# Gate products of the even layer as three fp32r products, their operands split on ScalarE, GpSimd and VectorE; ring loads and two copies moved ahead

## The reference, cut to what matters

```python
uh = uf.reshape(bsz, seq, RG_HEADS, RG_HEAD_DIM)          # 8 heads of 128 channels
gates = jax.nn.sigmoid(jnp.einsum('bshi,ghij->gbshj', uh, gate_w) + gate_b)
r, i = gates[0], gates[1]                                  # for each of two directions
log_a = -RG_C * r * jax.nn.softplus(-lam)
a = jnp.exp(log_a)
b = jnp.sqrt(-jnp.expm1(2.0 * log_a)) * (i * uf)
h = scan(a, b)                                             # forward, and in reverse
ya = (h_forward + h_reverse) * silu(za)
yb = gb * centred_dwconv(gc * xb, sc_w) * silu(zb)
y = concatenate([ya, yb]) @ w_out
```

## Time and profile before

| | us |
|---|---|
| median of 3 runs | 2738.15 |
| lowest and highest run | 2737.18, 2739.89 |
| the profiled execution's own time | 2736.76 |
| its span, first to last instruction | 2734.9 |
| PE busy in the span | 2696.8 (99%) |
| POOL, DVE, ACT busy | 1624.7, 1356.1, 708.7 |

### The profile page before, as it was taken

One profiled execution on the slowest core, in us unless ns is written; L12 is line 12 of the kernel. 1 busy time (PEld: TensorE's weight loads), 2 busy tenths in 40 slices (PEclk: granted clock), 3 DMA queues, 4 the chain that ended last, 5 costly groups with the idle time before them and its releaser, 6 DMA issues.

```text
span 2734.9 us, 36055 instructions
## 1 busy us (share of the span) xinstructions
PE 2696.8 (99%) x13190; PEld 2166.0 (79%) x13190; DVE 1356.1 (50%) x1605; ACT 708.7 (26%) x1235; POOL 1624.7 (59%) x949
## 2 busy tenths in 40 slices
PE   9999999999999999999999999999999999999999
PEld 6777777877888888867888888788888766888887
DVE  7878824574432461176440454642246777543242
ACT  4443423343200110284210113310012476211010
POOL 5666755524665666603665665566666799566565
PEclk9999999999999999999999999999999999999999
DMA  4222222202332322301332332333232100233232
GB/s 180 101 97 91 89 93 86 84 24 75 94 115 77 98 95 93 93 8 47 93 110 83 100 100 92 124 100 113 80 100 92 55 1 2 85 100 115 77 98 87
DMA packets 62028, 235.58 MB, mean 86 GB/s; under 512 B 6880, under 2 KB 7008, under 8 KB 61792
## 3 DMA queue, kind: packets, MB, share of 16 engines
q1 hardware_dynamic: 61920, 234.14, 26.9%
HBM read 232.02 MB, written 2.10 MB: 86 GB/s over the span
## 4 chain that ended last, share of the span: by engine, by line
PE 80%; DVE 6%; POOL 4%; PEld 3%; ACT 2%; issue 2%; DVEq 1%; DMA 1%; PEldq 0%; POOLq 0%; ACTq 0%; SPq 0%
PE ps L364 23%; PE ps L366 23%; PE ps L365 23%; POOL arena L2458 4%; PE ps L388 1%; PE ps L382 1%; PE ps L383 1%; PE ps L1045 1%; PEld ps L712 1%; PEld ps L713 1%; PEld ps L714 1%; PE ps L1029 1%; POOL w_lo L334 0%; DVE w_tails L1828 0%; DMA ring<-in_even_in 0%
## 5 line engine op out<-in xcount | busy, mean ns | idle before, releaser
L334 POOL TENSOR_TENSOR w_lo<-ring,w_hi 128x1024 fp32r<-128x1024 f32 (+2 forms) x382 | 985.9, 2581 | 56.5 <-issue 3.1
L332 POOL CAST w_hi<-ring 128x1024 fp32r<-128x1024 f32 (+2 forms) x382 | 435.1, 1139 | 910.7 <-PE ps L366 724.8
L364 PE MATMUL ps<-hi,w_hi 128*128 128x512 f32 x2064 | 809.0, 392 | 5.3 <-POOL w_lo L334 2.4
L365 PE MATMUL ps<-lo,w_hi 128*128 128x512 f32 x2064 | 803.2, 389 | 0.0
L366 PE MATMUL ps<-hi,w_lo 128*128 128x512 f32 x2064 | 803.2, 389 | 0.0
L364 PEld LDWEIGHTS ps<-hi,w_hi 128*128 128x128 f32 x2064 | 387.4, 188 | 93.1 <-POOL w_lo L334 6.0
L365 PEld LDWEIGHTS ps<-lo,w_hi 128*128 128x128 f32 x2064 | 387.5, 188 | 81.9 <-issue 2.1
L366 PEld LDWEIGHTS ps<-hi,w_lo 128*128 128x128 f32 x2064 | 387.4, 188 | 80.8
L364 PE MATMUL ps<-hid_hi,w_hi 128*128 128x512 f32 x704 | 274.4, 390 | 0.0
L365 PE MATMUL ps<-hid_lo,w_hi 128*128 128x512 f32 x704 | 274.0, 389 | 0.0
L366 PE MATMUL ps<-hid_hi,w_lo 128*128 128x512 f32 x704 | 273.9, 389 | 0.0
(11 more groups left out here) (367 smaller groups left out, 3318.8 us busy)
## 6 DMA issues: line engine op xcount, KB each, us to landing
ring<-in_ffn_in SPq DMA_DIRECT2D x176, 512.0 KB, 3.6
ring<-in_even_in SPq DMA_DIRECT2D x48, 512.0 KB, 4.9
ring<-in_ffn_out SPq DMA_DIRECT2D x32, 768.0 KB, 4.3
ring<-in_ffn_out SPq DMA_DIRECT2D x32, 640.0 KB, 3.9
ring<-in_even_out SPq DMA_DIRECT2D x16, 512.0 KB, 3.6
ring<-in_sb_qk SPq DMA_DIRECT2D x12, 512.0 KB, 3.6
ring<-in_odd_v SPq DMA_DIRECT2D x8, 512.0 KB, 3.6
ring<-in_odd_r SPq DMA_DIRECT2D x8, 512.0 KB, 3.7
```

The lines of the kernel that those rows point to most:

```text
L332: nc.gpsimd.tensor_copy(high[:, j % 2, 0:cols], ring[:, j, 0:cols])
L334: nc.gpsimd.tensor_tensor(low[:, j % 2, 0:cols], ring[:, j, 0:cols], high[:, j % 2, 0:cols].bitcast(F32), ALU.subtract).then_inc(sem["w_re ...
L364: nc.tensor.matmul(bank, w_hi[:, j % 2, w], x_hi[:, k, :], start=(k == 0), stop=False)
L365: nc.tensor.matmul(bank, w_hi[:, j % 2, w], x_lo[:, k, :], start=False, stop=False)
```

## The change

Three things are done, all in the even layer.

1. **Weights ahead of gate tiles.** In SP's loop the wait for `even_channel_done` and the load of the gate tile move from ahead of a channel's six slots to behind the fourth (`n == RING`).
2. **Two copies ahead of the roots.** In the first channel ACT moves banks 2 and 3 for the second channel (its `xa` and `xb`) ahead of the first channel's two square roots instead of behind them.
3. **Gates as three fp32r products.** ACT rounds the gate tile (`gw_hi`, 128x512) one channel ahead, and rounds `ua` (`ua_hi`, 128x512) behind its move of the fifth bank. POOL subtracts to get `gw_lo`, in two halves of 128x256, each behind a split of a slot. DVE subtracts to get `ua_lo` (128x512), behind the first instruction of the other branch (in the last channel directly behind `ua`, in the first behind its extra work). PE then has 12 fp32r matmuls per channel instead of 4 with unrounded operands, and waits for `ua_low` and for both halves (`gates_split`).

The core of the diff:

```diff
@@ -425,6 +425,12 @@
         nsp = r.take(16)
         nsp_c = r.tiles(2, 2)
         lt = r.tiles(6, 16)
+        r.at = (r.at + P - 1) // P * P
+        gw_hi = [at(f"gw_hi_{jj}", 4 * P, start, F32R) for jj, start in enumerate((ARENA_AT + r.at, place["root"]))]
+        r.take(4 * P)
+        gw_lo = tiled("gw_lo", 2, GATE_COLS, ARENA_AT + 16 * T, F32R)
+        ua_hi = at("ua_hi", T, place["acc"], F32R)
+        ua_lo = at("ua_lo", T, place["ring"] + 3 * SLOT + 8 * P, F32R)
         even_tmp = [ps[:, 4 + d, :] for d in range(2)]
         rinv_even = ps[:, 6, :]
 
@@ -612,10 +618,11 @@
                     with sp.Fori(0, RG_HEADS // 2 - 1) as i:
                         for jj in range(2):
 
-                            sp.wait_ge(sem["even_channel_done"], 2 * i + (jj + 3))
-                            gate_weight(i + 1, jj)
                             for n in range(6):
                                 s = 6 * jj + n
+                                if n == RING:
+                                    sp.wait_ge(sem["even_channel_done"], 2 * i + (jj + 3))
+                                    gate_weight(i + 1, jj)
                                 sp.wait_ge(sem["w_ready"], 12 * i + (s + 13))
                                 even_weight(i + 1, s)
                     continue
@@ -657,12 +664,14 @@
 
             def even_gates(i, jj):
 
-                pe.wait_ge(sem["ua_ready"], 2 * i + (jj + 1))
+                pe.wait_ge(sem["gates_split"], 4 * i + (2 * jj + 2))
                 pe.wait_ge(sem["gates_read"], 2 * i + (jj + 1))
-                pe.wait_ge(gate_landed[jj], 16 * i + 16)
+                pe.wait_ge(sem["ua_low"], 2 * i + (jj + 1))
                 for g in range(4):
-                    mm = nc.tensor.matmul(ps[:, 4 + g, :], gw[:, jj, g * P:(g + 1) * P], ua[:, jj, :],
-                                          start=True, stop=True)
+                    w = slice(g * P, (g + 1) * P)
+                    nc.tensor.matmul(ps[:, 4 + g, :], gw_hi[jj][:, w], ua_hi[:, :], start=True, stop=False)
+                    nc.tensor.matmul(ps[:, 4 + g, :], gw_lo[:, jj, w], ua_hi[:, :], start=False, stop=False)
+                    mm = nc.tensor.matmul(ps[:, 4 + g, :], gw_hi[jj][:, w], ua_lo[:, :], start=False, stop=True)
                 mm.then_inc(sem["gates_done"], 1)
 
             def even_channel(i, jj, c=None):
@@ -1311,18 +1320,28 @@
             rinv_act(act, "even_pre")
             nc.scalar.activation(rinv_even, root[:, :], ACT.Exp, scale=-0.5).then_inc(sem["rinv_copied"], 1)
 
+            def even_move(i, jj, n, c=None):
+                dst, func = [(xa_pad[:, jj, 2:2 + T], ACT.Copy), (xb_s[:, jj, :], ACT.Copy), (gc_s[:, jj, :], ACT.Copy),
+                             (gb_s[:, jj, :], ACT.Copy), (szb[:, jj, :], ACT.Silu), (sza[:, jj, :], ACT.Silu)][n]
+                s = 6 * jj + n
+                if c == 0:
+                    act.wait_ge(sem["plain_scaled"], n + 1)
+                else:
+                    act.wait_ge(sem["slots_used"], 12 * i + used("even_in", s + 1))
+                nc.scalar.activation(dst, ps[:, s % RING, :], func).then_inc(sem["even_moved"], 1)
+
+            def gates_high_act(i, jj):
+                act.wait_ge(gate_landed[jj], 16 * i + 16)
+                nc.scalar.activation(gw_hi[jj][:, :], gw[:, jj, 0:4 * P], ACT.Copy).then_inc(sem["gates_high"], 1)
+
             def even_act(i, jj, c=None):
                 act.wait_ge(sem["even_channel_done"], 2 * i + (jj + 1))
 
-                dsts = [(xa_pad[:, jj, 2:2 + T], ACT.Copy), (xb_s[:, jj, :], ACT.Copy), (gc_s[:, jj, :], ACT.Copy),
-                        (gb_s[:, jj, :], ACT.Copy), (szb[:, jj, :], ACT.Silu), (sza[:, jj, :], ACT.Silu)]
-                for n, (dst, func) in enumerate(dsts):
-                    s = 6 * jj + n
-                    if c == 0:
-                        act.wait_ge(sem["plain_scaled"], n + 1)
-                    else:
-                        act.wait_ge(sem["slots_used"], 12 * i + used("even_in", s + 1))
-                    nc.scalar.activation(dst, ps[:, s % RING, :], func).then_inc(sem["even_moved"], 1)
+                for n in range(2 if c == 1 else 0, 6):
+                    even_move(i, jj, n, c)
+                    if n == (1 if c == 0 else 4):
+                        act.wait_ge(sem["ua_ready"], 2 * i + (jj + 1))
+                        nc.scalar.activation(ua_hi[:, :], ua[:, jj, :], ACT.Copy).then_inc(sem["ua_high"], 1)
                     if c == 0 and n == 3:
                         for k in range(DT):
                             act.wait_ge(sem["even_scaled"], k + 1)
@@ -1331,6 +1350,8 @@
                     y_highs(DT, 2 * DT - 1)
                     act.wait_ge(sem["even_channel_done"], 1 + RG_HEADS)
                     y_highs(0, DT - 1)
+                else:
+                    gates_high_act(i + jj, 1 - jj)
                 par = gw[:, jj, 4 * P:4 * P + 16]
                 act.wait_ge(sem["gates_done"], 2 * i + (jj + 1))
                 for d in range(2):
@@ -1347,6 +1368,9 @@
                 for d in range(2):
                     a = nc.scalar.activation(hg[d], rg[d], ACT.Tanh, scale=nsp_c[:, jj, d:d + 1])
                 a.then_inc(sem["decay_ready"], 1)
+                if c == 0:
+                    even_move(0, 1, 0)
+                    even_move(0, 1, 1)
                 if c == RG_HEADS - 1:
                     act.wait_ge(sem["yb_done"], 1)
                     y_highs(2 * DT - 1, 2 * DT)
@@ -1359,6 +1383,7 @@
                     x_hi = hi[:, k, :] if k < DT else lo[:, k - DT, :]
                     nc.scalar.activation(x_hi, y_even[:, k, :], ACT.Copy).then_inc(sem["y_high"], 1)
 
+            gates_high_act(0, 0)
             for jj in range(2):
                 even_act(0, jj, jj)
             with act.Fori(0, RG_HEADS // 2 - 2) as i:
@@ -1768,6 +1793,10 @@
                 if c != 0:
                     V.tensor_copy(nsp_c[:, jj, :], nsp2[:, 2 * i + jj, :])
 
+                def ua_lower():
+                    dve.wait_ge(sem["ua_high"], 2 * i + (jj + 1))
+                    V.tensor_tensor(ua_lo[:, :], ua[:, jj, :], ua_hi[:, :].bitcast(F32), ALU.subtract).then_inc(sem["ua_low"], 1)
+
                 scale_plain(0)
                 scale_plain(1)
                 moved(1)
@@ -1777,11 +1806,14 @@
                     op = V.scalar_tensor_tensor(ua[:, jj, :], xa_pad[:, jj, k:k + T], par[:, 4 + k:5 + k],
                                                 ua[:, jj, :], ALU.mult, ALU.add)
                 op.then_inc(sem["ua_ready"], 1)
+                if c == RG_HEADS - 1:
+                    ua_lower()
 
                 if c == 0:
                     scale_plain(2)
                     scale_plain(3)
                     normed(0, DT)
+                    ua_lower()
                     scale_plain(4)
                     scale_plain(5)
                     decay_terms((11, 9, 7, 5, 3, 1))
@@ -1800,6 +1832,8 @@
                 moved(3)
                 V.tensor_tensor(u_pad[:, 1:1 + T], gc_s[:, jj, :], xb_s[:, jj, :], ALU.mult)
                 dve.drain()
+                if c not in (0, RG_HEADS - 1):
+                    ua_lower()
                 V.tensor_scalar(cv, u_pad[:, 0:T], par[:, 9:10], None, ALU.mult)
                 for k in range(1, 3):
                     dve.drain()
@@ -2388,9 +2422,22 @@
             pool.wait_ge(sem["w_ready"], ready("even_in", 1))
             for j in range(1, RING):
                 split_slot(pool, "even_in", 0, j)
-            with pool.Fori(0, slots_of["even_in"] // RING - 1) as i:
-                for j in range(RING):
-                    split_slot(pool, "even_in", i + 1, j)
+            def split_gates(i, jj, half):
+                w = slice(2 * P * half, 2 * P * half + 2 * P)
+                pool.wait_ge(sem["gates_high"], 2 * i + (jj + 1))
+                pool.sem_inc(sem["split_begun"], 1)
+                nc.gpsimd.tensor_tensor(gw_lo[:, jj, w], gw[:, jj, w], gw_hi[jj][:, w].bitcast(F32), ALU.subtract)\
+                    .then_inc(sem["gates_split"], 1)
+
+            for s in range(RING, 12):
+                split_slot(pool, "even_in", s // RING, s % RING)
+                if s in (5, 6, 10, 11):
+                    split_gates(0, s // 8, s % 5 % 2)
+            with pool.Fori(0, RG_HEADS // 2 - 1) as i:
+                for s in range(12):
+                    split_slot(pool, "even_in", 3 * i + (3 + s // RING), s % RING)
+                    if s % 6 in (2, 3):
+                        split_gates(i + 1, s // 6, s % 6 - 2)
             pool.wait_ge(sem["consts_landed"], 16)
             for dst, name in ((ident_1, "ident"), (causal_1, "causal_neg"), (sb_neg_1, "sb_neg"), (neg_c_1, "neg_c")):
                 G.tensor_copy(dst, con(name))
```

(2 more changed lines are left out.)

## The result

The changed kernel takes 2783.82 us (median of 5 runs, 2783.44 to 2784.86), against 2738.22 for the kernel before, timed beside it: a ratio of 1.0167, 95% interval 1.0156 to 1.0178. It is 45.6 us slower. The forecast said slower by 17; its range ended at 2771.

The account below looks back on a forecast made before the run. PE bounds the kernel, with DVE, alternating with POOL, a second clock. Stretches +9.2, -0.2, +6.5, +2.0 and last gates -0.4 gave +17.1 on 2736.76, 2753.9; with 1.4 for the median, 2755 us, slower by 0.6%; range 2739 to 2771.

Parts of the forecast that it names:

- PE, 2.72 us for the gates: Gate products on PE: 12 matmuls take 2.72 us against 3.44, 0.72 less per channel, 5.8 in all.
- SP: Wait moved behind the fourth slot: ring stays full, removing PE's waits for `w_lo` (2.2 and three of 0.5).
- The two copies count nothing: First stretch: copies remove its 1.6 us stall, but DVE holds the second gate start; counted nothing, bound 0 to 1.6.
- ACT's copy of the gate tile is free: ACT's gate-tile copy falls into its wait for the gates, free; if ACT were full, 0.60 us a channel.
- The halves, 0.7: POOL's two halves per channel delay DVE by 0 to 1.2 us; 0.7 taken.
- the 35.8 of the forecast: Steady period: `ua` ready 35.8 us behind the gate start, from 33.64, gates -0.72, a fifth slot subtraction 2.2, halves 0.7.
- First stretch 41.5: First to second gate start: 41.5 us through added DVE and POOL work, against 32.3, so +9.2.
- Steady period 38.1: Later gate starts 38.1 us apart by DVE's path; PE, ready at 35.4, waits 2.7 in every channel.
- rival D: One collision more: POOL's next-slot subtraction also precedes `ua_lo`, 2.3 us more in six periods, 13.8: 2769; chance 0.17.
- No term for the clock: Ahead of each gate call: PE waits 2.7 us, counted with no charge for the clock.
- The estimate made from it: Gates on PE: four passes at this pace give 3.63 us, gain 0.91 a channel, 7.3 in all; sum used the row's 3.44.

Follow-up runs that it names:

- e6: Changed kernel with 20 spare matmuls ahead of PE's wait for `ua_lo` in channels 1 to 6: 2771.65 us against 2737.47, ratio 1.0117.
- e1: Kernel before with only SP's wait and gate-tile load moved behind the fourth slot: 2741.87 us against 2737.47, ratio 1.0016.
- e2: Kernel before with only ACT's two copies of channel 1 moved behind the decay of channel 0: 2737.96 us against 2737.47, ratio 1.0000.
- e11: Changed kernel without the move of ACT's two copies, both other parts kept: 2781.37 us (2 runs), ratio 1.0158.
- e4: Changed kernel without POOL's two gate halves from channel 2 on, PE multiplying by `gw_hi` instead: 2752.11 us (2 runs), ratio 1.0050.
- e5: Changed kernel without DVE's subtraction that makes `ua_lo` in channels 2 to 5, semaphore raised in its place: 2767.75 us (2 runs), ratio 1.0107.
- e7: Changed kernel with `ua_lo` directly behind `ua` in every channel but the first: 2768.23 us (2 runs), ratio 1.0109.
- e8: e7 with POOL starting the first slot of a channel only behind `ua_ready`: 2741.20 us against 2738.32 (11 runs), ratio 1.0009.
- e10: e8 with the cast of a channel's first slot on ACT and POOL's subtraction behind `ua_lo`, replacing the `ua_ready` waits: 2739.37 us against 2737.43, ratio 1.0006.
- e9: Kernel before, unrounded gates, with weights ahead, copies ahead and POOL's two waits for `ua_ready`: 2735.59 us against 2737.43 (11 runs), ratio 0.9991.
- e12: e10 with ACT's cast also for the output projection's first slot, and 20 spare matmuls ahead of the second gate start: 2735.66 us against 2737.91, ratio 0.9991.
- e3: Changed kernel with SP's wait and the copies put back, so only the three-product gates are new: 2741.16 us against 2737.47, ratio 1.0012.

## Why the prediction was wrong in size

The direction was right, and so was the place. The sum was short by 29.9 us (2783.82 against 2753.9 for the profiled execution). By its own steps:

- *PE, 2.72 us for the gates*: near right wherever the clock was up (2.72 in the first channel, 2.88 from 177.61 to 180.49 in e6), but 4.2 to 5.3 in the changed kernel's other channels.
- *SP*: right. The ring is full and the waits for `w_lo` are gone (e1).
- *The two copies count nothing*: right as far as e2 and e11 can tell.
- *ACT's copy of the gate tile is free*: no run speaks against it; the copy of `ua` took 0.63 us.
- *The halves, 0.7*: mis-sized. Their own length in alternation is 1.19 each (rows of after above), and they push `ua` back. `ua` came 36.55 us behind the gate start in e6 (173.31 less 136.76) and 35.09 without the halves in e4: they cost 1.46, over the upper bound of 1.2. Without them the forecast's sum is 35.1, and e4 meets it. The 0.7 us that the term was short decide more than their size, since they decide on which side of POOL's subtraction `ua_lo` falls. No run with the changed kernel's order of instructions has `ua` at the 35.8 of the forecast, so whether POOL's cast alone would have come first there is not shown.
- *First stretch 41.5*: 40.16 measured, the one term that erred to the other side.
- *Steady period 38.1*: this is the step that failed. The prediction put 2.3 us between `ua` and the gates: POOL's cast takes its turn ahead of `ua_lo`, its subtraction does not. Measured: 4.3 in e6 (173.31 to 177.61), and 3.7 or 4.3 behind the first stretch of the changed kernel (2.9 ahead of the last gates). DVE's product stands ahead of `ua_lo`, and in that time POOL gets its cast in and begins its subtraction, which then holds `ua_lo`, or the product ahead of it. This is rival D, which was given 0.17 and a period of 40.4; e6, where the clock is up in most stretches, has 40.85, and its median of 2771.65 stands beside D's 2769. e4, with `ua` 1.46 earlier, has the order that the forecast described: 2.44 between `ua` and the gates.
- *No term for the clock*: the prediction charged PE's waits at their own length. It had foreseen PE idle for 2.7 us ahead of every gate call and did not ask what this does to the matmuls behind. (The six waits of nearly that length, 2.3 to 2.6 in e5 and e7, lowered nothing; the collision made them 4.7 to 5.5.) With 5 us of idle time the gates ran at 1.2 GHz, DVE's chain, which waits for the gates, resumed 10.8 to 11.9 instead of 9.4 to 9.5 us behind the gate start, and periods became 41.9 to 43.8. e6 against the changed kernel puts this at 12.2 us.

Added up: the six periods behind the first stretch took 257.6 us against 6 x 38.1 = 228.6, so 29.0 of the 29.9 are theirs. By e6 at least 12.2 are the clock's, which leaves 16.8 or less for the order of turns; e6's steady period gives the same (40.85 less 38.1, six times, is 16.5). The rest nearly cancels: first gate start +1.5, first stretch -1.3, end +0.8. One slip has no weight: PE's work without a stall is 247.2, not 247.3.

The Trainium skill, "SBUF — State Buffer", section "Who interferes with whom", has the rule that a VectorE and a GpSimd instruction of these kinds exclude each other; the trace agrees (0.69 becomes 2.65 in e6, and 1.13 beside a cast in e8). The prediction cited it and then counted one turn too few.

The other page that the prediction cited, the Trainium skill's "FP8 and Floating Point Precision", section "TensorE Precision Notes", has four passes for a true FP32 product. The estimate made from it, 3.63 for the gates and 0.91 less a period, came out too high: e10's period of 35.40 against e9's 36.12 gives 0.72, as the row had it.

The first gate start lies at 51.5 to 51.7 in five profiled executions (before, e2, e9, e11, e12) and at 53.0 to 53.3 in the other nine; e10 and e12 lie on different sides and do the same ahead of it. The difference is the clock's: between 14 and 20 us it is 1.00 in the five and 0.72 to 0.79 in the nine, whose matmuls start 0.43 us apart for a while. e10, then e12:

```profile
14.00:20.00 6.00, 6.00 (x21) 4.72 (x20) 5.59 (x9) 2.02 (x5) 0.00 (x0) 0.72 1.05 436
14.00:20.00 6.00, 6.00 (x28) 4.90 (x27) 5.63 (x9) 2.71 (x5) 0.24 (x1) 1.00 1.09 456
```

So the +1.5 us ahead of the first gates are no effect of the change: executions that do the same differ by them. Open is why the clock fell there in some executions and not in others, when all fourteen have PE waiting 1.8 us just ahead (to about 13.5 or 14), and why one wait of 1.90 us in e4 lowered it and four did not.

## To carry to other kernels

Where two engines take turns, as DVE and POOL do here, an engine that starves for data may be shielding the other: before a late transfer is made punctual, find out what runs undisturbed in the gap, and keep it by an explicit wait (here two lines of waits gave back 27.0 us, and with `ua_lo` moved ahead 42.6 of 45.6). Write down the order of turns around the instruction that releases the critical engine, for both sides of every near tie, since one more turn is a whole instruction of the other engine. And a wait of the matmul engine has to be priced with the clock behind it, since slow matmuls delay whatever waits for them.

## What the runs showed of the hardware that was not expected

- One wait of 5 us in 43 was enough for the 1.2 GHz level. In the runs with three-product gates each of the 26 waits of 4.66 us or more ahead of the gates was followed by 5 to 13 matmuls at 0.43 us instead of 0.23, and the six of 2.3 to 2.6 us (e5, e7) by none; but of six waits of 1.90 us (e4, e3) two were, so no simple rule follows from these rows.
- 20 matmuls of no use, put into such a wait, made the kernel 12 us faster (e6): the slow gates delay DVE's chain, and the chain the next gates.
- DVE and POOL alternate instruction by instruction even where both are short: a half, of 0.60 us by the earlier trace rows, took 1.18 to 1.20 beside DVE's work in 14 of 16 cases of the changed kernel (151.15 and, in the next slot, 156.59), and 0.73 and 0.75 in the first two.
